# Gate tiles of the selected-key mixer: each behind its own head pair's values, their rounding in one group

## Chip, cores and metric

One Trainium2 chip, one core. The metric is the time on the device in microseconds (us); lower is better. Three runs of the kernel before are given.

## What is computed

The model has two stages for one sequence of 512 positions and width 1024. The first (two layers of convolution, dilated attention, a gated recurrence, and a feed-forward network) is not touched. The second has two layers (l = 0, 1), each of which is cut here to what matters:

```python
z = u @ w_in                                   # u: the normed, modulated input; w_in 1024 x 8772
ya = dsa_attention(rope(aq), rope(ak), av, rope(iq), rope(ik), iw)   # 8 heads of 64; each query keeps the best 128 keys
ya = ya.reshape(bsz, seq, 512) * silu(ag)      # mixer "a": selected keys, gated
yb = swa_sinks_attention(...) * silu(bg)       # mixer "b": window of 128 keys, with sinks
yc = stick_breaking_attention(...) * silu(cg)  # mixer "c"
merged = (sigmoid(ma) * (ya @ w_br_a) + sigmoid(mb) * (yb @ w_br_b) + sigmoid(mc) * (yc @ w_br_c))
x = x + gate * (merged @ w_out)
```

The change concerns `* silu(ag)` in both layers: when its four column tiles are multiplied by TensorE, and when their product with the attention's output is rounded for the next multiplication.

## The kernel before

Activations lie transposed, 128 features on the partitions and all 512 positions along the row. Every large product is made in three fp32 matmuls per 128 x 128 block of weights (line 573, called from `thrice`): high part of the weights by the high and the low part of the input, and low part of the weights by the high part. A chunk of weights (1024 x 256) comes by DMA into one of two buffers `raw` (`sync_program`), ScalarE rounds it into `wh` and VectorE subtracts that from it into `wl`; there are two pairs of those.

The order of all work is one list of units, made in Python before the program is written (`make_order`). Each engine's program walks that list and issues its share of each unit, so all queues run in that order, and semaphores keep the data right. Within a layer of the second stage the list comes from `Order.weave` (line 408): it holds a list of **main** units, which keep their order (tiles of the large products), and several lists of **side** units (attention). At each step it takes a side unit whose conditions are met and whose modelled time has come; otherwise the next part of the main tile in work; and if the next main tile has an unmet condition of its own, only side units. It has a modelled clock per engine (`COST`, `COST_BY_KEYS`), which decides the order and nothing else.

The main units of a layer follow `BLOCK2`. Around the change, for layer 0: ... bkv, bq0, bq1, an0, ag0, ag1, an1, ap0, ap1, am2, am3, bn0, bn1, bn2, bg0, bg1, .... Here `an0` is two tiles of the merge gate of mixer a (`mg`), `ag0` and `ag1` two gate tiles each (`gate`, four in all, c = 0 to 3), `ap` and `am` tiles of `ya @ w_br_a` (`br`) and more merge gates, `bn` merge gates of mixer b, `bg` gate tiles of mixer b. In layer 1 the tiles of bq stand earlier, ahead of mixer c's gates; the rest is the same.

The side units of mixers a and b come from `head_steps` (line 2139), for four head pairs c = 0 to 3 and four query blocks i = 0 to 3 each:

- `s1` scores on TensorE (the rows ps<-ak,aq or ps<-bk,bq), then bias and maximum on VectorE; at most two tiles are in flight (s1 waits for s2 of two tiles before);
- `sx` exponent on ScalarE, `sn` normalizing on VectorE;
- `s2` transposes on TensorE (line 786, ps<-cst_r,s), copied out by ScalarE into `pt`;
- `s3` values on TensorE (ps<-pt,av or ps<-pt,bv), copied by ScalarE over the queries (`aq`, `bq`), which becomes `y`.

Query block i of mixer a looks at i + 1 key blocks, of mixer b at one or two. The sides of mixer b may begin only once `("s3", "a", l, 3, 3)` is done, the last values of mixer a.

A gate tile (`gate`) takes 24 matmuls 128x512 in four parts on TensorE; ScalarE takes tanh into a buffer `rawt` (two of them, `raw_slot`); VectorE makes (tanh + 1) times the tile, and multiplies y by it. That last product waits for `("att", "a", l, c)`. The unit `gs` (`mixer_split`) rounds the gated row: ScalarE writes its high part over the keys `ak` (and waits for the last scores of mixer a, which read them), VectorE writes the low part `aq_r` over y. The tiles `br` need all four rows. The gate tiles of mixer b (`bg`) wait in the planner for the last values of mixer b, `("s3", "b", l, 3, 3)`.

Before, all four gate tiles of mixer a have the condition `("s3", "a", l, 3, 3)`, and `gs` of a tile goes into `late`, which puts it behind the next main tile.

Of the kernel before, what the change touches and what calls it, by code (L numbers as in the profile page):

```python
# [2138 lines left out]
def head_steps(cfg, l, n, first, bias=False):  # L2139

    scores, rest, tiles = [], [], [(c, i) for c in range(n) for i in range(NT)]
    for x, (c, i) in enumerate(tiles):
        if bias and i == 0:
            scores.append((("gb", l, c), [("s1", cfg, l, c - 1, NT - 1)] if c else []))
        after = first(c) + ([("gb", l, c)] if bias else [])
        scores.append((("s1", cfg, l, c, i), after + ([("s2", cfg, l) + tiles[x - 2]] if x > 1 else [])))
        scores.append((("sx", cfg, l, c, i), None))
        rest.append((("sn", cfg, l, c, i), [("sx", cfg, l, c, i)]))
        rest.append((("s2", cfg, l, c, i), None))
        rest.append((("s3", cfg, l, c, i), None))  # L2150
    return scores, rest
# [96 lines left out]
def order_early(o, tag, key, before):  # L2248


    j = o.use(key, True)
    o.put("early", tag, j, 0, 1)
    for k in (KD - 2, KD - 1):
        o.put("sq", norm_before(tag), k)
        o.put("er", tag, k)
    o.put("early", tag, j, 1, KD)
    while o.split_one():
        pass
    o.put("rms", tag)
    o.put("mod", tag, before)  # L2260
    o.put("ed", tag)
    while o.split_one():
        pass
    o.put("em", tag)
    return j


def order_out(o, which, l):
    o.put("banks", (0, 1, 2, 3), (4, 5, 6))
    o.sums()  # L2270
    o.put("lnexp")
    tag, norm = ("o1" if which == 1 else "o3", l), ("m2", l) if which == 1 else ("m3", 1) if l == 0 else ("fin2", 0)
    n, more = 0, norm != ("fin2", 0)
    if more:
        o.put("es", norm)
    for c in range(4):
        j = o.use(("out", which, l, c))
        for os in [(0, 1)] if c == 0 else [(2 * c,), (2 * c + 1,)]:
            o.put("out", which, l, tag, os, j)
            while n < os[-1] and not (more and n == KD - 2):  # L2280
                o.put("sq", norm, n)
                if more:
                    o.put("er", norm, n)
                n += 1
    if not more:
        o.put("sq", norm, n)
# [69 lines left out]
def order_block2(o, l):  # L2356
    j = order_early(o, ("m3", l), ("iq", l), ("o3", 0) if l else ("m2", 1))
    for c in range(2):
        o.put("rope", l, "iq", c, 128 * c, 128, j)
    if l == 0:  # L2360
        o.put("rms", ("fin", 0))
    o.put("banks", (0, 1), (3, 7))
    mains, late = [], [("rest", l, "iq", 0), ("rest", l, "iq", 1)]
    held = [("iw", l), ("rest", l, "ik", 0), ("ikc", l)]
    finals = [("final", ("fin", 0), "fin", k, k + 1) for k in range(KD)] if l == 0 else []
    wide = ("banks", (0, 1, 2), (3, 7, 4, 5, 6))

    def main(units, parts, key=None, after=None):

        mains.append((units, parts, key, after))  # L2370
        while late:
            mains.append(([late.pop(0)], 1, False, None))
        if finals and units[0][0] == "v2":
            mains.append(([finals.pop(0)], 1, False, None))

    def tiles(units, parts, key, after=None):
        for n, unit in enumerate(units):
            main([unit], parts, None if n else key, None if n else after)

    def rope(nm, c, key, n=128, after=None):  # L2380
        main([("rope", l, nm, c, 128 * (c % 2), n)], 4, key, after)
        late.append(("rest", l, nm, c))

    for chunk in BLOCK2[l][1:]:
        nm, x = (chunk[:-1], int(chunk[-1])) if chunk[-1].isdigit() else (chunk, 0)
        if nm in ("cq", "ck"):
            tiles([("cqk", l, nm, 2 * x + c) for c in range(2)], 4, (nm, l, x))
            if held:
                mains += [([held.pop(0)], 1, False, None) for _ in range(3)]
        elif nm in ("cv", "av"):  # L2390
            tiles([("v2", l, nm, x, tb) for tb in range(NT)], 2, (nm, l, x))
        elif nm in ("aq", "ak", "bq"):
            for c in range(2):
                rope(nm, 2 * x + c, (nm, l, x) if c == 0 else None)
        elif nm == "ik":
            main([("rope", l, "ik", 0, 0, 68)], 4, ("ik", l))
        elif nm == "bkv":
            rope("bk", 0, ("bkv", l), after=[("tr", l, 3, 15, 16)])
            main([("bv", l)], 4)
            late += [("bkc", l), ("bvt", l)]  # L2400
        elif nm[1] == "g":
            for c in (2 * x, 2 * x + 1):
                main([("gate", l, nm[0], c)], 4, (nm, l, x) if c % 2 == 0 else None, [wide] if nm == "cg" else [("s3", nm[0], l, 3, 3)])
                late.append(("gs", l, nm[0], c))
        else:
            if nm[1] != "p":
                tiles([("mg", l, nm[0], 2 * x + c) for c in range(2)], 4, (nm[0] + "m", l, x))
            while late and nm[1] == "p":
                mains.append(([late.pop(0)], 1, False, None))
            if nm[1] != "n":  # L2410
                tiles([("br", l, nm[0], 2 * x + c) for c in range(2)], 2, (nm[0] + "br", l, x))

    side_c, side_d = [], []
    steps = [(c, u) for c in range(4) for u in range(3)]
    for n, (c, u) in enumerate(steps):
        side_c.append((("c1", l, c, u), [("cqk", l, "ck", c)] + ([("c2", l) + steps[n - 2]] if n > 1 else [])))
        side_c.append((("ch", l, c, u), [("c1", l, c, u)] + ([("c3", l) + steps[n - 2]] if n > 1 else [])))
        side_d.append((("c2", l, c, u), [("ch", l, c, u)]))
        side_d.append((("c3", l, c, u), [("c2", l, c, u), ("v2", l, "cv", 1, 3)]))
    side_d.append((wide, None))  # L2420
    index, last = [], []
    for i in range(1, NT):
        index += [(("ts", l, i, h), [("ikc", l)] + last) for h in range(4)] + [(("tm", l, i), None)]
        index += [(("tr", l, i, r, r + 1), None) for r in range(16)]
    sides = [side_c, side_d, index]
    for cfg in "ab":
        first = [("tr", l, 3, 15, 16), wide, ("v2", l, "av", 1, 3)] if cfg == "a" else [("bkc", l), ("bvt", l), ("s3", "a", l, 3, 3)]
        sides += head_steps(cfg, l, 4, lambda c, first=first: first)
    o.weave(mains, *sides, ahead=AHEAD2, weight=WEIGHT2, behind=BEHIND)
    order_rows3(o, l)  # L2430
    order_out(o, 2, l)


def order_rows3(o, l):
    for k in range(KD):
        o.put("row", ("o3", l), k)


def make_order(o, first):
    o.put("start")  # L2440
    o.put("adaqp", 0)
    for k in range(KD):
        o.put("sqf", ("m1", 0), k)
    o.put("rms", ("m1", 0))
    for l in range(2):
        order_block1(o, l)
        order_ffn(o, l)
    for l in range(2):
        order_block2(o, l)
    o.put("rms", ("fin2", 0))  # L2450
    o.put("final", ("fin2", 0), "fin2")
    assert o.split == len(o.plan) and not o.late
    return o.units
# [214 lines left out]
```

## Time and profile before

| what | us |
|---|---|
| median of 3 runs | 2777.92 |
| lowest, highest | 2770.64, 4207.18 |
| span of the profiled execution | 2769.2 |
| TensorE busy (matmul records) | 2666.7 |
| VectorE, ScalarE, GpSimd busy | 1855.3, 1153.6, 696.7 |
| layer 0 of the second stage, mixer a's last eight tiles without main work | 34.35 of the span |

No time of its own is listed for the profiled execution beside its span; the lowest run is 1.4 above the span, which is taken for what lies around it. A matmul's record is longer than the distance to the next one, since they are pipelined, so work is read from the distance between the starts. A "granted clock" of 1.00 is 2.4 GHz, 0.50 is 1.2 GHz.

### The profile page before, as it was taken

The numbers are of one execution on the slowest core, as the hardware profiler recorded it, in microseconds if no ns is written. First come the engines' busy times: TensorE is split into PE (matmuls) and PEld (weight loads), VectorE is DVE, ScalarE is ACT, GpSimd is POOL, SyncE is SP. The second block draws the span as 40 slices with busy tenths as digits, with TensorE's granted clock in tenths as the row PEclk, the third lists the DMA queues.
The fourth block names the chain that finished last, engine by engine and source line by source line (L and its number), as shares of the span: only waits on it lengthen the run. The fifth ranks groups of instructions, "written<-read, shape, count | busy, mean of one in ns | idle before, by whom it ended". The sixth has DMA issues, their size and how long they took to land.

```text
span 2769.2 us, 36817 instructions
## 1 busy us (share of the span) xinstructions
PE 2666.7 (96%) x14748; PEld 2135.3 (77%) x14748; DVE 1855.3 (67%) x3088; ACT 1153.6 (42%) x1900; POOL 696.7 (25%) x514
## 2 busy tenths in 40 slices
PE   6999999999999998999999999999999999999997
PEld 5877677888878776787887888776787788777776
DVE  7789668876677775877467868745546548644544
ACT  3243644333242454443224464344434564444432
POOL 0000046998800003365550031000100122000100
PEclk9999999999999998999999999999999999999999
DMA  8443033554432112344442534231223322222322
GB/s 275 123 145 105 30 122 130 168 182 159 153 113 69 60 60 71 121 152 140 149 131 88 179 105 151 84 96 32 91 64 108 96 65 83 88 81 68 94 66 77
DMA packets 281115, 302.58 MB, mean 109 GB/s; under 512 B 9969, under 2 KB 263025, under 8 KB 280945
## 3 DMA queue, kind: packets, MB, share of 16 engines
q1 hardware_dynamic: 267568, 250.21, 29.0%
q0 software_dynamic: 13088, 49.55, 5.4%
q8 instruction: 117, 1.92, 0.3%
q10 hardware_dynamic: 288, 0.47, 0.1%
q14 instruction: 54, 0.43, 0.0%
HBM read 289.97 MB, written 2.10 MB: 105 GB/s over the span
## 4 chain that ended last, share of the span: by engine, by line
PE 85%; DVE 9%; ACT 4%; issue 1%; DMA 1%; SPq 0%; DVEq 0%; ACTq 0%
PE ps L573 82%; PE ps L786 2%; DVE wl L1420 1%; DVE hl L1426 1%; DVE adaacc L1426 1%; DMA raw<-in_w_in 1%; DVE ca L1426 1%; ACT wh L944 1%; DVE recat L1725 0%; ACT hh L944 0%; ACT recat L944 0%; DVE rawt L1426 0%; ACT att_p L944 0%; DVE uv L1426 0%; DMA stage<-in_w_ada 0%
## 5 line engine op out<-in xcount | busy, mean ns | idle before, releaser
L573 PE MATMUL ps<-hh,wh 128*128 128x512 f32 x2208 | 887.4, 402 | 18.8 <-DVE wl L1420 10.7
L573 PE MATMUL ps<-hh,wl 128*128 128x512 f32 x2208 | 864.0, 391 | 0.0
L573 PE MATMUL ps<-hl,wh 128*128 128x512 f32 x2208 | 862.9, 391 | 0.0
L1420 DVE TENSOR_TENSOR wl<-raw,wh 128x2048 fp32r<-128x2048 f32 (+3 forms) x234 | 478.1, 2052 | 143.6 <-ACT wh L944 143.3
L573 PEld LDWEIGHTS ps<-hh,wh 128*128 128x128 f32 x2208 | 414.7, 188 | 133.6 <-issue 40.0
L573 PEld LDWEIGHTS ps<-hh,wl 128*128 128x128 f32 x2208 | 414.9, 188 | 91.2
L573 PEld LDWEIGHTS ps<-hl,wh 128*128 128x128 f32 x2208 | 415.6, 188 | 79.6
L944 ACT ACTIVATE wh<-raw 128x2048 fp32r<-128x2048 f32 (+3 forms) x234 | 370.1, 1592 | 223.4 <-PE ps L573 196.2
L573 PE MATMUL ps<-fh,wh 128*128 128x512 f32 x432 | 172.1, 398 | 2.5 <-DVE wl L1420 2.5
L573 PE MATMUL ps<-fh,wl 128*128 128x512 f32 x432 | 169.0, 391 | 0.0
L573 PE MATMUL ps<-fl,wh 128*128 128x512 f32 x432 | 168.9, 391 | 0.0
L1993 POOL TENSOR_TENSOR strewn<-strewn,cond 128x1024 f32<-128x1024 f32 x80 | 163.5, 2044 | 8.2 <-DMA strewn<-in_w_ada 6.5
L1426 DVE SCALAR_TENSOR_TENSOR xT<-ps,mod,xT 128x512 f32<-128x512 f32 x80 | 59.5, 748 | 135.3 <-PE ps L573 135.2
L1995 POOL TENSOR_TENSOR strewn<-strewn 128x512 f32<-128x512 f32 x84 | 145.6, 1733 | 6.6
L1952 POOL DMA_DIRECT2D gbias<-in_gb x6 | 3.5, 577 | 542.0 <-DVE stt L1423 447.3
L573 PE MATMUL ps<-wh,hh 128*128 128x256 f32 x448 | 128.7, 287 | 3.4 <-DVE apad L1420 3.4
L573 PE MATMUL ps<-wl,hh 128*128 128x256 f32 x448 | 126.7, 283 | 0.0
L573 PE MATMUL ps<-wh,hl 128*128 128x256 f32 x448 | 126.7, 283 | 0.0
L573 PEld LDWEIGHTS ps<-recq,reck 64*128 64x128 f32 x1536 | 100.8, 201 | 26.5 <-issue 14.8
L573 PE MATMUL ps<-recq,reck 64*128 64x64 f32 (+2 forms) x1536 | 110.4, 296 | 5.0 <-DVE reck L1420 3.1
L944 ACT ACTIVATE rawt<-ps 128x512 f32<-128x512 f32 (+1 forms) x82 | 48.7, 597 | 148.4 <-PE ps L573 148.3
L1976 POOL DMA_DIRECT2D strewn<-in_w_ada x80 | 63.1, 788 | 157.6 <-PE ps L573 132.4
(304 smaller groups left out, 4199.3 us busy)
## 6 DMA issues: line engine op xcount, KB each, us to landing
raw<-in_w_in SPq DMA_DIRECT2D x75, 1024.0 KB, 5.3
raw<-in_w_up SPq DMA_DIRECT2D x46, 1024.0 KB, 5.1
strewn<-in_w_ada POOLq DMA_DIRECT2D x80, 512.0 KB, 4.1
raw<-in_w_ada SPq DMA_DIRECT2D x24, 1024.0 KB, 5.3
raw<-in_w_in SPq DMA_DIRECT2D x44, 512.0 KB, 5.1
raw<-in_w_out SPq DMA_DIRECT2D x16, 1024.0 KB, 5.1
raw<-in_w_down SPq DMA_DIRECT2D x16, 1024.0 KB, 5.2
stage<-in_w_ada SPq DMA_DIRECT2D x8, 1024.0 KB, 11.7
```

The source lines that it names most:

```text
L573: return e.matmul(o, a, b, start=start, stop=stop, skip_group_check=True)
L786: m = e.transpose(b[:, o:o + 128], S[:, 128 * x:128 * x + 128], M.ident)
L944: return e.activation(o, a, f, **k)
L1420: return e.tensor_tensor(o, a, b, op)
L1426: return e.scalar_tensor_tensor(out=o, in0=a, scalar=s, in1=b, op0=op0, op1=op1)
L1952: e.dma_start(M.Gb[h], X.T["gb"][2 * c + h, :, :]).then_inc(*X.tally.up16("bias_in", ("bias", l, c)))
L1976: e.dma_start(M.strewn[h][:, :, c:c + n], src[:, 4 * h:4 * h + 4, :]).then_inc(*X.tally.up16(f"strewn_in{h}", ("strewn", j, h)))
L1993: e.tensor_tensor(v, v, weights, ALU.mult).then_inc(*up("pool_ada"))
L1995: e.tensor_tensor(v[:, 0:2, :], v[:, 0:2, :], v[:, 2:4, :], ALU.add).then_inc(*up("pool_ada"))
```

## The change

The planner's condition of gate tile c of mixer a is no longer the last values of the whole mixer but those of its own head pair c, `("s3", "a", l, c, 3)`. The units `gs` of mixer a no longer go one behind each next tile: they are held and put in one group of four behind the fourth gate tile, with the condition `("s3", "a", l, 3, 3)`. Mixers b and c are as before. No instruction is added or removed; only the order of the list differs.

```diff
             for c in (2 * x, 2 * x + 1):
-                main([("gate", l, nm[0], c)], 4, (nm, l, x) if c % 2 == 0 else None, [wide] if nm == "cg" else [("s3", nm[0], l, 3, 3)])
-                late.append(("gs", l, nm[0], c))
+                main([("gate", l, nm[0], c)], 4, (nm, l, x) if c % 2 == 0 else None,
+                     [wide] if nm == "cg" else [("s3", nm[0], l, c if nm == "ag" else 3, 3)])
+                if nm == "ag":
+                    held.append(("gs", l, "a", c))
+                else:
+                    late.append(("gs", l, nm[0], c))
+            if nm == "ag" and x == 1:
+                mains.append(([held.pop(0)], 1, False, [("s3", "a", l, 3, 3)]))
+                mains += [([held.pop(0)], 1, False, None) for _ in range(3)]
```

## Rows read from the trace of the kernel before

**Rows 1.** The page, part 1: busy time of the engines

```profile
PE 2666.7 (96%) x14748; PEld 2135.3 (77%) x14748; DVE 1855.3 (67%) x3088; ACT 1153.6 (42%) x1900; POOL 696.7 (25%) x514
```

**Rows 2.** Stretches: length, busy of each engine, clock, DMA share, GB/s

```profile
1820.43:1857.07 36.64, 36.64 (x201) 27.91 (x200) 20.14 (x48) 17.64 (x39) 5.16 (x4) 1.00 0.39 115
1860.79:1895.14 34.35, 26.00 (x166) 15.45 (x165) 15.27 (x67) 16.88 (x49) 0.00 (x0) 0.75 0.00 1
1895.14:2031.99 136.85, 136.68 (x708) 103.53 (x706) 68.42 (x214) 59.18 (x149) 11.26 (x8) 1.00 0.25 78
2365.00:2506.99 141.99, 141.99 (x770) 107.88 (x768) 71.59 (x175) 62.97 (x133) 4.52 (x3) 1.00 0.26 80
2506.99:2653.67 146.68, 145.28 (x749) 110.74 (x747) 72.15 (x214) 63.20 (x156) 12.20 (x8) 1.00 0.25 79
1867.00:1876.00 9.00, 7.78 (x39) 4.56 (x38) 3.97 (x18) 3.96 (x12) 0.00 (x0) 0.50 0.00 0
```

**Rows 3.** TensorE in time, layer 0, mixer a with main tiles between: start, length

```profile
1842.20 1.13 PE L573 MATMUL ps<-ak,aq 64*128 64x512 f32 x4
1843.26 0.66 PE L573 MATMUL ps<-pt,av 128*64 128x128 f32 x8
1843.85 0.50 PE L573 MATMUL ps<-hh,wh 128*128 128x512 f32 x1
...
1857.07 1.03 PE L786 MATMUL ps<-cst_r,s 128*128 128x128 f32 x8
1857.86 0.48 PE L573 MATMUL ps<-hh,wh 128*128 128x512 f32 x1
```

**Rows 4.** TensorE in time, layer 0, mixer a with no main tile

```profile
1860.79 0.70 PE L573 MATMUL ps<-ak,aq 64*128 64x256 f32 x4
...
1866.55 1.15 PE L786 MATMUL ps<-cst_r,s 128*128 128x128 f32 x4 [1.54 <-DVE s L1423]
1867.63 2.08 PE L573 MATMUL ps<-ak,aq 64*128 64x512 f32 x4
...
1888.13 1.07 PE L786 MATMUL ps<-cst_r,s 128*128 128x128 f32 x6 [1.37 <-DVE s L1423]
...
1894.11 1.09 PE L573 MATMUL ps<-pt,av 128*64 128x128 f32 x16 [0.69 <-ACT pt L944]
1895.14 0.50 PE L573 MATMUL ps<-hh,wh 128*128 128x512 f32 x1
```

**Rows 5.** TensorE's waits from 1860.8 to 1895.2

```profile
PE ps L786 <- DVE s L1423: 6.5, 6, 1.5
PE ps L573 <- ACT pt L944: 1.7, 3, 0.8
```

**Rows 6.** Layer 0: last values of mixer b; ScalarE empties the main tile before gate b

```profile
2031.41 0.66 PE L573 MATMUL ps<-pt,bv 128*64 128x128 f32 x8
...
2033.68 0.60 ACT L944 ACTIVATE ak<-ps 128x512 f32<-128x512 f32 x1 [1.30 <-PE ps L573]
```

**Rows 7.** Layer 1: mixer b's last tile on TensorE

```profile
2646.51 0.70 PE L573 MATMUL ps<-bk,bq 64*128 64x256 f32 x4
...
2651.69 0.70 PE L786 MATMUL ps<-cst_r,s 128*128 128x128 f32 x4 [0.72 <-DVE s L1423]
2653.08 0.66 PE L573 MATMUL ps<-pt,bv 128*64 128x128 f32 x8 [0.69 <-ACT pt L944]
2653.67 0.50 PE L573 MATMUL ps<-hh,wh 128*128 128x512 f32 x1
```

**Rows 8.** VectorE: gate products of mixer b, layer 1, one tile each

```profile
2666.24 0.69 DVE L1420 TENSOR_TENSOR bq<-bq,rawt 128x512 f32<-128x512 f32 x1
...
2671.68 0.69 DVE L1420 TENSOR_TENSOR bq<-bq,rawt 128x512 f32<-128x512 f32 x1
```

**Rows 9.** ScalarE in layer 1: last tile before the gates, gate 0, first rounding

```profile
2515.24 0.60 ACT L944 ACTIVATE cq<-ps 128x512 f32<-128x512 f32 x1 [3.37 <-PE ps L573]
...
2522.37 0.58 ACT L944 ACTIVATE rawt<-ps 128x512 f32<-128x512 f32 x1
...
2531.99 0.61 ACT L944 ACTIVATE ak_r<-aq 128x512 fp32r<-128x512 f32 x1
```

## The prediction

> **What bounds the kernel now.** I read the page's busy times first: TensorE's records cover 96% of the span and no other engine more than 67% [rows 1]. So an order of work pays only where TensorE's share is broken. Next I cut the second stage into stretches and looked where TensorE's busy time falls short of the length [rows 2]. In layer 1 the stretch of mixer a (2365.00 to 2506.99) is full, and that of mixer b lacks 1.4 us in 146.68. In layer 0 mixer b's stretch lacks 0.2 us in 136.85. The one real hole is in layer 0, from 1860.79 to 1895.14: 26.00 us busy in 34.35, with a mean clock of 0.75 and no DMA.
>
> The order of TensorE in time shows what that hole is [rows 4]: between the scores of pair 2, block 1 and the first matmul of gate tile 0 no main tile stands at all. The planner had used up its main tiles, and the next one (gate 0) was held for the last values of mixer a. The waits inside are the attention's own chain: 6.5 us on VectorE's normalizing and 1.7 us on ScalarE's copy of the transposes [rows 5].
>
> **What the hole is worth.** Work at full clock is read from starts in the covered stretch just before [rows 3]: scores of four key blocks take 1843.26 - 1842.20 = 1.06 us, 0.265 a key block; 8 value matmuls take 0.59, 0.074 each; 8 transposes take 0.79, 0.099 each. The hole holds scores over 2+3+4+1+2+3+4 = 19 key blocks (5.0 us), 96 value matmuls (7.1) and 40 transposes (3.9): 16.0 us. So 34.35 - 16.0 = 18.3 us of the hole is excess, in eight tiles of attention, 2.3 us a tile. Of it 8.35 is plain idle time; the other 10 is mostly the low clock: from 1867 to 1876 the granted clock was 0.50, which is 1.2 GHz [rows 2], and the scores that took 1.13 us in the covered stretch took 2.08 [rows 3, 4].
>
> The busy share would say that only those 8.35 us are to be had. The Trainium skill (Perfetto Trace Analysis, Identifying the Most-Contended Engine) says that matmul busy time is a poor measure of a full TensorE, and that the busy time of the weight loads is the better one. By it the covered stretch has 27.91 us of weight loads in 36.64 and the hole 15.45 in 34.35, so the hole holds 20.3 us of work and 14.1 us of excess. That is between my two counts and nearer to the one by starts.
>
> **The change, part by part.**
>
> *Gates 0 and 1 go into the hole.* Their pairs are finished when it begins. A gate tile is 5.44 us of TensorE (distance between two gate products when nothing stands between them [rows 8]), so 10.9 us of main work becomes available. It doesn't slip into idle time alone. With a main tile open the planner puts parts of it between all steps of the attention. From 1820.43 to 1857.07, the transposes of the last blocks of pairs 0 and 1, four tiles of attention took 36.64 us [rows 2], of which their own work is 10 x 0.265 + 40 x 0.074 + 20 x 0.099 = 7.6; so a tile consumes (36.64 - 7.6) / 4 = 7.3 us of main work. Gates 0 and 1 then cover 10.9 / 7.3 = 1.5 tiles.
>
> *Gate 2 goes in too, a little later,* once pair 2's values are done, in the middle of the hole: 5.44 / 7.3 = 0.75 of a tile. Gate 3 waits for the same unit as before. Together 2.25 of the eight tiles get covered and 5.75 stay bare: the gain is 2.25 x 2.3 = 5.2 us. From both sides: if every part fell into a hole and kept the clock up, all of 3 x 5.44 = 16.3 us would be gained (less than the excess of 18.3). If the weight split that comes with each chunk (about 2 us each on ScalarE and VectorE) and the two extra VectorE operations of a gate tile (0.69 each [rows 8]) delay the attention as much as the cover gives, nothing is gained. I take 5.2, since the rate of 7.3 us a tile is what this planner did with the same attention in the same layer.
>
> *Mixer b in layer 0 loses that cover.* The same three tiles were the first main work of mixer b's stretch, 16.3 us of it. Mixer b's attention begins behind the last values of a, as before, and the next fence is bg, which waits for the last values of b. Before, the main tile ahead of gate b ended about 2033.5, when ScalarE took it, 1.5 us behind mixer b's last values (2031.41 + 0.6) [rows 6]. So main tiles now run out 16.3 - 1.5 = 14.8 us too early. Mixer b used up main work at this rate: 136.85 us for 16 tiles [rows 2], a tile's own work being about 1.4 (scores of 1.75 key blocks 0.46, 7 values 0.52, 3.5 transposes 0.35, rounded up for their first loads), leaves 7.1 a tile. So 2.1 tiles of mixer b become bare. The price: layer 1 shows b's last tile nearly bare. From its scores to the end of its values 7.16 us pass (2646.51 to 2653.67), with 2.7 us of main parts and 1.4 us of idle time in it [rows 7]; without those parts about 4.1 us would have been idle. For 2.1 tiles I take 4.1 + 0.5 = 4.6 us. Bounds: 2 us (if mixer b moves faster, since the gate tiles' VectorE work has left its beginning) and 10 us (if the clock falls there as in the hole, 14.8 / 7.1 x 2.3 = 4.8, doubled).
>
> *The group of four roundings.* Nothing is added: four copies on ScalarE (0.61 [rows 9]) and four subtractions on VectorE. But in the new order the fourth follows directly on gate 3. ScalarE's copy must wait for tanh (0.58), the two VectorE products (0.69 each) and then blocks its queue, and VectorE waits in turn for the copy; behind them stand exponents and normalizing of mixer b's first tiles. That is about 2.5 us during which no attention of b advances, and TensorE has a merge-gate tile of 5.44 us in hand. Cost 0 to 2 us a layer; I take 0.5 for both together. The tiles `br`, which need all rows, come two tiles (10.9 us) later, enough.
>
> *Layer 1.* The condition moved doesn't bind there: gate 0 began after ScalarE took the tile ahead of it, about 2515 [rows 9], 8 us behind mixer a's last values at 2506.99. So nothing moves except the roundings. A shift there can change the 1.4 us of idle time at the end of b either way [rows 7]; I take 0.
>
> *DMA, loads and queues.* The splits of ag1 and an1 come some 20 us earlier. SyncE's queue waits for the split before it loads, so loads come earlier as well; the DMA share is 0.00 in the hole, so there is room [rows 2]. No other queue is passed.
>
> **Sum.** -5.2 + 4.6 + 0.5 + 0 = -0.1, and the low clock: the hole's bare pieces are shorter (three tiles at most in a row), so part of its 10 us of low clock may go; I take -1.9 for that. Together -2.0 us. The profiled execution has 2769.2 of span and, by the lowest run, 1.4 around it: 2770.6. The two runs that lie together are 2770.64 and 2777.92; a new median falls between rather than at the lowest, so I count from their middle, 2774.3. Forecast 2772. The point is that the kernel had one supply of main tiles before bg, and the change spends it earlier; the hole moves from the end of mixer a to the end of mixer b, and only the difference in price is won.
>
> **Rivals.**
>
> *The hole is filled and not moved* (-5 to -12 us, about 2765). If the parts fill idle time, 16.3 us are won in mixer a, and the loss in b stays 4.6. For it: TensorE waits in pieces of at most 1.54 us [rows 4], and a part of 1.36 us fits into such a piece. Also, the Trainium skill (same page, Optimization Strategy) advises to interleave stretches with different limits. Against it: the planner spent 7.3 us of main work a tile where 2.3 would do.
>
> *Mixer b is starved at a higher price* (+5 us, about 2779). Place: the end of mixer b in layer 0, just ahead of gate b. The shortage of 14.8 us leaves 2.1 to 2.5 tiles bare with the clock at 0.50 and costs 10 us, while mixer a gains 5.2. It decides from the point where the bare end of b costs more than the hole gives, 5.2. For it: in the hole the clock was at 0.50 by 1867, 6 us behind the last main matmul [rows 2]. Against: mixer b's tiles are short, one or two key blocks.
>
> *The change doesn't do what it says* (0, about 2774). The planner's modelled clock could put all attention of a first, if its units are always due. Against: between 1820 and 1857 it did interleave.
>
> *The grouped roundings stall mixer b in both layers* (+2 to +4, about 2777), by the chain worked out above. That can be told by VectorE's and ScalarE's waits behind gate 3.
>
> **How the numbers follow.** The forecast with its surroundings (-6 to +2) 0.50; filled 0.20; starved 0.12; does nothing 0.08; roundings 0.10. Two in ten left out reach from -11 to +7, so from 2774 the range is 2762 to 2781; it also takes in that the base itself is known to 4 us. 2% of this kernel is 55 us, about what a measurement can tell from no change; all cases lie far inside that. Faster by over 2% gets 0.01, slower 0.01.
>
> **What would show it.** Right: in layer 0 gate matmuls (128x512) stand between scores of pair 2 and 3 of mixer a; the stretch from pair 2, block 1 to the last values grows from 34 to about 45 us, still with about 8 us of idle time or low clock more than the covered stretch; mixer b's stretch shrinks to about 125 us, with 4 to 5 us idle in its last 10. Layer 1's order on TensorE before the gates is the same, and four roundings stand in a row behind gate 3. Wrong: idle time in mixer a's stretch under 3 us (filled), or over 8 us at the end of mixer b (starved), or a change outside layer 0 of the second stage.

## The result: 5 us slower, and the profile after

The changed kernel takes 2779.23 us (median of 20 runs, 2769.56 to 2783.61) against 2772.94 for the kernel before (20 runs). The ratio, in which the one run before of 4207.18 us does not count, is 1.0018, with a 95% interval of 1.001 to 1.0027: about 5 us slower, clear of no change, far inside 2%. The forecast was 2 us faster. The time lies in the stated range; the direction is wrong.

The spans of two profiled executions differ by more (2780.8 and 2769.2), and that difference can't be taken whole: the first scores of mixer a in layer 0, ahead of which no kernel of this study differs, begin anywhere from 1775.6 to 1786.4 us in the traces. So all readings below are distances within one trace, between instructions that every kernel here has. The first, called mixer a's tail, goes from the transposes of pair 1's last block in mixer a, layer 0, to the end of mixer a's last values; the second on to the end of mixer b's last values; the third on to the fourth gate product of mixer b.

| stretch of layer 0, us | before | after | main work moved in or out | gain (+), loss (-) |
|---|---|---|---|---|
| mixer a's last eight tiles | 38.07 | 53.98 | +16.33 (72 matmuls) | +0.4 |
| mixer b | 136.85 | 126.38 | -14.97 (66) | -4.5 |
| to the fourth gate product | 24.81 | 24.67 | -1.36 (6) | -1.2 |
| sum | 199.73 | 205.03 | 0 | -5.3 |

The six matmuls of the third row are the part of the main tile ahead of gate b that ran behind mixer b's last values before. Mixer b and the row behind it lose 5.7 us together. The 1.2 us behind mixer b are low clock: the granted clock is 0.95 there and was 1.00, and the first matmuls behind the bare end stand 0.43 us apart where 0.23 is usual.

From the fourth gate product of layer 0 to the end of mixer a in layer 1 it is 450.2 us in both, and from there to layer 1's fourth gate product 170.1 in both. The 5.3 us are the whole effect in the traces, and they agree with the ratio.

The same view of stretches as [rows 2], of the kernel after: mixer a's tail, mixer b in layer 0, mixer b in layer 1, and two pieces of mixer a's tail (length, busy of each engine, clock).

```profile
1863.48:1917.46 53.98, 46.44 (x257) 32.77 (x256) 23.78 (x76) 23.66 (x57) 0.00 (x0) 0.80 0.06 20
1917.46:2043.84 126.38, 122.82 (x642) 92.32 (x640) 62.63 (x205) 54.42 (x144) 10.29 (x8) 0.99 0.24 76
2518.68:2665.34 146.66, 145.25 (x748) 110.71 (x746) 71.76 (x214) 63.29 (x156) 12.20 (x8) 1.00 0.25 79
1887.00:1892.00 5.00, 4.98 (x30) 3.69 (x28) 1.79 (x9) 2.84 (x10) 0.00 (x0) 0.50 0.00 0
1904.00:1920.00 16.00, 13.45 (x64) 8.87 (x63) 3.82 (x14) 5.72 (x15) 0.00 (x0) 0.50 0.01 1
```

Mixer a's tail is still 7.5 us short of busy, though 16.3 us of work went in; its clock is 0.80, where the same eight tiles had 0.78 before. Mixer b in layer 0, nearly full before, now lacks 3.6. Layer 1 is as it was.

TensorE's waits in mixer a's tail after, against [rows 5] (who waited for whom, total, times, longest):

```profile
PE ps L786 <- DVE s L1423: 6.2, 3, 2.5
PE ps L573 <- ACT pt L944: 1.4, 2, 0.7
```

Three waits for VectorE's normalizing add up to nearly what six did before. TensorE in time shows where the longest two stand, and ahead of them a tile that did not wait.

```profile
1874.43 0.38 PE L786 MATMUL ps<-cst_r,s 128*128 128x128 f32 x2
...
1876.13 0.92 PE L573 MATMUL ps<-ak,aq 64*128 64x384 f32 x4
1876.98 0.44 PE L573 MATMUL ps<-pt,av 128*64 128x128 f32 x4
1877.35 0.50 PE L573 MATMUL ps<-hh,wh 128*128 128x512 f32 x1
...
1880.21 0.60 PE L786 MATMUL ps<-cst_r,s 128*128 128x128 f32 x4
1880.57 0.48 PE L573 MATMUL ps<-hh,wh 128*128 128x512 f32 x1
...
1882.13 0.66 PE L573 MATMUL ps<-pt,av 128*64 128x128 f32 x8
1882.72 1.13 PE L573 MATMUL ps<-ak,aq 64*128 64x512 f32 x4
1886.28 1.54 PE L786 MATMUL ps<-cst_r,s 128*128 128x128 f32 x6 [2.43 <-DVE s L1423]
...
1895.55 0.38 PE L786 MATMUL ps<-cst_r,s 128*128 128x128 f32 x2
1895.69 0.48 PE L573 MATMUL ps<-hh,wh 128*128 128x512 f32 x1
...
1899.99 0.44 PE L573 MATMUL ps<-pt,av 128*64 128x128 f32 x4
1900.36 0.92 PE L573 MATMUL ps<-ak,aq 64*128 64x384 f32 x4
1903.81 1.15 PE L786 MATMUL ps<-cst_r,s 128*128 128x128 f32 x4 [2.53 <-DVE s L1423]
```

In the two groups with the long waits, read from above: transposes of a tile, gate matmuls (6 in the first, 18 in the second), values, scores of the tile two further on, and only then the wait. Nothing of the gate is left to stand in it. The tile at 1874.43 is of the same size as the one at 1895.55 and also has 18 gate matmuls, but 12 of them stand behind its scores and values (from 1877.35), and the next transposes (1880.21) follow without a wait.

What VectorE does ahead of the last of these waits, the one that ends at 1903.81 (bias and maximum of the scores from 1900.36, then normalizing of the tile that TensorE waits for):

```profile
1900.73 0.69 DVE L1426 SCALAR_TENSOR_TENSOR rawt<-rawt,ps 128x512 f32<-128x512 f32 x1 [1.96 <-ACT rawt L944]
1901.45 0.69 DVE L1420 TENSOR_TENSOR aq<-aq,rawt 128x512 f32<-128x512 f32 x1
1902.06 0.55 DVE L1764 CUSTOM_DVE_ANT_0 s<-ps,sel 128x384 f32<-128x384 f32 x1
...
1903.40 0.35 DVE L1423 TENSOR_SCALAR s<-s,stt 128x256 f32<-128x256 f32 x1
```

So the normalizing comes behind the newest scores, and the two products of a gate tile stand ahead of both. At the end of mixer b the last two tiles are bare, with 3.5 us of waits (forecast: 2.1 tiles, 4 to 5 us idle):

```profile
2037.29 0.70 PE L573 MATMUL ps<-bk,bq 64*128 64x256 f32 x4
2038.04 0.66 PE L573 MATMUL ps<-pt,bv 128*64 128x128 f32 x8
2041.52 0.70 PE L786 MATMUL ps<-cst_r,s 128*128 128x128 f32 x4 [2.82 <-DVE s L1423]
2042.91 1.00 PE L573 MATMUL ps<-pt,bv 128*64 128x128 f32 x8 [0.69 <-ACT pt L944]
```

### The profile page after: what moved, and what is told of

Read it like the earlier page. It is cut to its first block, busy times and chain, and to the rows that moved or that the text cites. A ratio compares the mean times of both kernels' runs of the same rounds, so it can differ in the third digit from the quotient of the medians.

```text
span 2780.8 us, 36816 instructions
## 1 busy us (share of the span) xinstructions
PE 2675.6 (96%) x14748; PEld 2143.2 (77%) x14748; DVE 1856.2 (67%) x3088; ACT 1154.0 (41%) x1900; POOL 697.7 (25%) x514
## 4 chain that ended last, share of the span: by engine, by line
PE 85%; DVE 9%; ACT 3%; issue 1%; DMA 1%; SPq 0%; DVEq 0%; ACTq 0%
PE ps L573 83%; PE ps L786 2%; DVE wl L1420 1%; DVE hl L1426 1%; DVE adaacc L1426 1%; DVE ca L1426 1%; DVE recat L1725 1%; DMA raw<-in_w_in 0%; ACT wh L944 0%; DVE rawt L1426 0%; ACT recat L944 0%; DMA stage<-in_w_ada 0%; DVE uv L1426 0%; ACT hh L944 0%; DVE reck L1420 0%
## 6 DMA issues: line engine op xcount, KB each, us to landing
stage<-in_w_ada SPq DMA_DIRECT2D x8, 1024.0 KB, 11.6
```

## The experiments

The three stretches of layer 0 for every kernel, read in its one trace between the same instructions. The kernels e1, e2, e4, e8, e11 and e12 ran once each, so for them there is no comparison of whole times:

| kernel | mixer a's tail | mixer b | to gate product 4 | sum |
|---|---|---|---|---|
| before | 38.07 | 136.85 | 24.81 | 199.73 |
| after | 53.98 | 126.38 | 24.67 | 205.03 |
| e1 group only | 37.08 | 137.71 | 24.81 | 199.60 |
| e2 two gates | 47.42 | 133.34 | 24.44 | 205.20 |
| e4 short vector | 51.82 | 125.94 | 25.90 | 203.66 |
| e5 spare, after | 53.46 | 125.71 | 25.31 | 204.48 |
| e6 spare, before | 35.52 | 136.88 | 24.80 | 197.20 |
| e7 own pair b, after | 53.88 | 133.39 | 12.57 | 199.84 |
| e8 own pair b, before | 37.03 | 137.83 | 24.80 | 199.66 |
| e9 = e8 + spare | 35.52 | 136.86 | 24.80 | 197.18 |
| e10 = e7 + spare in bare tiles | 50.88 | 132.18 | 12.57 | 195.63 |
| e11 = e12 + e4 | 50.08 | 125.69 | 24.99 | 200.76 |
| e12 spare in bare tiles, after | 50.87 | 125.71 | 24.75 | 201.33 |
| e13 parts in the waits | 40.10 | 128.85 | 25.17 | 194.12 |
| e14 = e13 + own pair b | 40.11 | 135.43 | 12.57 | 188.11 |

(e3 moves other work through these stretches and is read below.)

**Which part of the change costs.** e1 keeps the grouped roundings and undoes the condition:

```diff
-                     [wide] if nm == "cg" else [("s3", nm[0], l, c if nm == "ag" else 3, 3)])
+                     [wide] if nm == "cg" else [("s3", nm[0], l, 3, 3)])
```

> Only the grouped roundings of the change; the gate tiles wait for all of mixer a, as before. Measure: layer 0, from the transposes of pair 1's last block (mixer a) to the last gate product of mixer b: 199.7 us before, 205.0 after. If the whole loss comes from the moved condition, this run shows 199.7 (within 0.3) and the same 38.1 us for mixer a's last eight tiles. If the grouped roundings stall mixer b, it shows 201 to 203, with new waits of TensorE behind gate 3.

Measured: 199.60, the kernel before. Mixer a's tail took 37.08 here and 37.03 in e8, which both have the TensorE order of the kernel before in it, against 38.07 there; mixer b took 0.9 more. So the sums are the safer number, and the tail of a single trace is good to 1 us. Against these two tails the change's +0.4 in mixer a would be -0.6, and its loss behind it 4.7: nothing was gained in mixer a, by either reading. The roundings cost nothing.

e2 lets only gates 0 and 1 go ahead (`c if nm == "ag" and c < 2 else 3`).

> The change, but only gates 0 and 1 may go ahead of mixer a's end; gates 2 and 3 wait for its last values. Theory cheap tiles and low clock (the price of a bare tile is not 2.3 us for each; cover put on short blocks saves little, and bare rows of tiles left cost more at 1.2 GHz): mixer a's stretch (38.1 before, 54.0 after, of which 16.3 are the three gates) is 38.1 + 10.9 - 1 = 48, and mixer b's end loses a third less, so the whole stretch is 201.5 to 203. Rival, the even price of my prediction: mixer a's stretch 38.1 + 10.9 - 3.5 = 45.5, the whole 199 to 200.

Measured: mixer a's tail 47.42, so the 10.9 us of gates 0 and 1 gained 1.5 there (0.5 against the tails of e1 and e8). The third gate tile then gained nothing: it adds 6.56 to the tail and is 5.44 long. The sum, though, is 205.20, as bad as with three gates and over the range that I gave: 10.9 us of main work are taken out behind mixer a, 9.5 of them (42 matmuls) from mixer b's stretch, and only 3.9 us are saved, 3.5 of them in mixer b. That is a loss of 7.0, where three gates lost 5.7. The price at the end of b doesn't go by how much cover is missing. The planner spent what was left faster: the last main part began about 10 us ahead of the end of b's values, and about 8 us with three gates. Here the granted clock was 0.97 in b's stretch (0.99 after), and the last group of four transposes, at 2032.76, took 1.12 us where 0.60 is usual. The stretch:

```profile
1902.36:2035.70 133.34, 129.65 (x666) 97.53 (x664) 65.21 (x209) 56.58 (x147) 13.19 (x8) 0.97 0.24 76
```

**Is mixer b's loss the missing supply?** e3 puts the two tiles bn3 ahead of bg:

```diff
-           "bn0", "bn1", "bn2", "bg0", "bg1", "bn3", "bp0", "bp1", "bp2", "bp3")] * 2
+           "bn0", "bn1", "bn2", "bn3", "bg0", "bg1", "bp0", "bp1", "bp2", "bp3")] * 2
```

> The change, and the last two merge-gate tiles of mixer b (bn3, 10.9 us of main work) put ahead of the gate tiles bg in both layers, so that mixer b's end has cover again. Theory (the loss in mixer b is the missing supply of main tiles ahead of bg): the 3.5 us idle at the end of b in layer 0 fall under 1 and those in layer 1 (1.4) to 0; against the kernel after 4 to 6 us less, so about equal to the kernel before or 1 below. Rival (the work moved forward is missed further back, or the planner spends it earlier just the same): idle time stays at 3 to 4 us, or appears ahead of the tiles bp, and the time is that of the kernel after.

Measured: ratio to the kernel before 0.9997 (0.9985 to 1.0009), so level with it. The idle time at the end of b went from 3.5 to 0 in layer 0 and from 1.4 to 0 in layer 1. With bn3's 10.9 us taken off, layer 0's sum is 199.9. But behind the gates, where bn3 had stood, time is lost: the way to layer 1's mixer a is 1.9 us longer (bn3 taken off), and so is the end of layer 1 by 1.8. Both theory and rival hold in part.

e7 gives mixer b's gates the same own-pair condition (`c, 3)` for all), on top of the change; e8 does that to the kernel before.

> The change, and the gate tiles of mixer b too wait for their own pair's values only, in both layers (their roundings stay where they are). Supply theory: mixer b's end is covered by its gates 0 to 2, so its stretch in layer 0 loses 4 to 5 us against the kernel after (idle 3.5 to under 1), layer 1 loses its 1.4; whole kernel level with the kernel before, within 2 us. Rival: the gates of b are spent in the same way and leave the last tiles bare again, idle at the end of b stays above 2 us.

> The kernel before with mixer b's gate tiles behind their own pairs. Layer 0 has cover to the end of b before, so its stretches stay (199.7 us); layer 1 loses the 1.4 us idle at the end of b. If more changes, the gates' condition has a price or gain of its own.

Measured: e7 0.9995 (0.9984 to 1.0006), and its mixer b in layer 0 has no gap left:

```profile
1910.64:2044.03 133.39, 133.39 (x690) 100.99 (x688) 66.14 (x208) 57.30 (x147) 10.29 (x8) 0.99 0.24 76
```

Its sum is 199.84, with mixer a's tail as in the kernel after (53.88), so 5.2 of the 5.3 us are back, and layer 1 gains 1.7 (168.43 for 170.12). e8 leaves layer 0 alone (199.66) and gains the same 1.7 in layer 1. The loss in mixer b was the missing supply of main tiles ahead of bg.

**Why mixer a gained nothing: VectorE, clock, or place.** e4 shortens VectorE's work of the gates and the weights' rounding:

```diff
+            if p["key"] in (("ag", 0, 1), ("am", 0, 1)):
+                c1 = c0 + 16
...
+        n = 16 if l == 0 and nm == "a" and c < 3 else 512
-        tt(y, y, raw, ALU.mult).then_inc(*up("dve_gate", ("gated", l, nm, c)))
+        tt(y[:, 0:n], y[:, 0:n], raw[:, 0:n], ALU.mult).then_inc(*up("dve_gate", ("gated", l, nm, c)))
```

> The change, but in layer 0 the VectorE products of gate tiles 0 to 2 and the rounding of the weights of ag1 and an1 work on 16 columns only (most of these values are left out); order and waits stay. Theory VectorE in the way (gate products of 0.69 us each and a split of 2.3 stand in the queue ahead of the attention's maximum and normalizing): TensorE's waits of 2.4 and 2.5 us in mixer a's stretch fall to 1.5 or less and the stretch from 54.0 to 50 to 51.5. Rival (low clock and cheap tiles only): the stretch stays at 53 to 54.

Measured: 51.82, 2.2 us less; the waits for VectorE fell only from 6.2 to 5.3, the longest to 2.2. That is a part of the loss; the stretch ends just over the 50 to 51.5 of the theory. By the sum it is 1.4 us less (203.66), since the stretch to the fourth gate product took 25.90 for 24.67.

e5, e6 and e12 add spare matmuls so that TensorE's clock stays up:

```diff
+    def spare(cfg, l, c, b, n):
+        if cfg == "a" and l == 0 and c > 1:
+            for _ in range(n):
+                mm(b[:, :], M.cst_r[:, C_ID:C_ID + 128], M.hh[:, 0, :], True, True)
```

> The change, and in layer 0 for pairs 2 and 3 of mixer a spare matmuls (128x512, fp32r, into the bank just claimed, whose content the next instruction overwrites) ahead of the waits: 5 before a tile's transposes (1 for the first block), 2 before its values. They add no result. Theory low clock (the bare tiles of the kernel after cost more since they run at 1.2 GHz): the granted clock stays at 1.00 through mixer a's stretch, which falls from 54.0 to 48 to 50 us, and mixer b's first main part is no longer slow. Rival (bare tiles are bound by VectorE and ScalarE, and the clock costs little): the stretch stays at 53 to 55, since TensorE has to wait for them all the same.

> The same spare matmuls in the kernel before. Low clock theory: mixer a's last eight tiles take 30 to 33 us and not 38.1, so this kernel gains 5 us or more, which says how much of the hole was the clock's. Rival: 37 to 39.

> The change, with the spare matmuls (5 ahead of the transposes, 2 ahead of the values) only in the five tiles of layer 0 that stand bare in it: pair 2, blocks 2 and 3, and pair 3, blocks 1 to 3. In the run with spare matmuls in all tiles mixer a's stretch was 53.5 us, with some 13 spare matmuls (3 us) among covered tiles. If the low clock is a part of the lost gain, the stretch is now 50 to 51 (54.0 without). If those 3 us were hidden before too and the clock is worth nothing, 53 to 54.

Measured: e5 53.46, as its rival had it; e6 35.52, between theory and rival; e12 50.87, as by its theory. The clock did stay up; the tail of e6 and of e12:

```profile
1855.28:1890.80 35.52, 34.81 (x233) 22.73 (x231) 15.28 (x67) 17.80 (x51) 0.00 (x0) 1.00 0.00 1
```

```profile
1853.90:1904.77 50.87, 48.08 (x292) 33.46 (x291) 23.80 (x76) 23.06 (x57) 0.00 (x0) 1.00 0.07 21
```

So the low clock was worth 2.5 us in the kernel before (I had booked up to 10 of its hole to it, and expected 5 here) and 3.1 in the kernel after (by the sums 2.5 and 3.7). In e5 the 13 spare matmuls among covered tiles cost 2.6 us of their own, the difference to e12. Over whole executions e6 is a little faster than before, 0.9987 (0.9976 to 0.9998); e5 is slower, 1.0025 (1.0014 to 1.0036).

> Both at once: the spare matmuls in the five bare tiles, and the VectorE products of gates 0 to 2 and the weights' rounding for ag1 and an1 on 16 columns (left out for most values). VectorE alone gave 51.8 us for mixer a's stretch. If clock and VectorE add up, 48 to 49, which is near what my even price gave (38.1 + 16.3 - 5.2 = 49.2); what is then missing to the 35.5 + 16.3 = 51.8 of the kernel before with spare matmuls is the true cover of the gates, 3 us or so. If they are one and the same loss, 50 to 51.

Measured: 50.08. Clock (3.1) and VectorE (2.2) don't add up: together they give 3.9. With the clock kept up on both sides, 35.52 + 16.33 = 51.85 is what no cover at all would give; the three gate tiles cover 1.0 us of their 16.3 (e12), 1.8 with short VectorE work as well, about what two traces can differ by. What was left open is why main work in a stretch full of waits hides in none.

e13 moves nothing into or out of layer 0 and changes the order within mixer a's tail: where the parts of gates 0 to 2 stand, how many stand together (one a tile, but two in the first), and that scores always come ahead of values, as in the kernel before. One tile of it, as a list of units and not as code:

```diff
 s2(2,3), s1(3,1), s3(2,3)
+part of gate 1
 sx(3,1), sn(3,0), s2(3,0), s1(3,2), s3(3,0)
+part of gate 1
 sn(3,1), sx(3,2), s2(3,1)
-(planner: part, s2(3,0), part, part, part, s3(3,0), s1(3,2), sn(3,1), s2(3,1))
```

> The change, but in layer 0 the list of mixer a's last eight tiles is written by hand: the attention in the order of the kernel before, and ten of the twelve parts of gates 0 to 2 one by one behind a tile's scores and values, ahead of the next transposes, where TensorE waits for VectorE. Theory place (in the kernel after, the parts stand ahead of scores(t+2), which VectorE works through before it normalizes tile t+1, so they lengthen the loop that TensorE waits on and do not fill the wait): with the parts behind the scores most of their 13.6 us are hidden; the whole stretch of layer 0 is 194 to 199 us (205.0 after, 199.7 before). Rival (attention with cover takes that long wherever the parts stand, because VectorE's extra work and the quantum of 1.4 us cost it): 203 to 206.

> The same, and mixer b's gates behind their own pairs. By the theories place and supply together the loss at the end of b (5 us) goes too: layer 0 189 to 194 us, layer 1 1.7 less; 7 to 11 us less than before, ratio 0.996 to 0.9975. If only supply holds: 199 to 200 and 1.7, ratio 0.999.

Measured: e13 0.9981 (0.997 to 0.9993), e14 0.9967 (0.9955 to 0.9978). The tail holds ten gate parts (60 matmuls, 13.6 us) and takes 40.10 us, 2.0 more than the kernel before without them: 11.6 us are hidden, and the clock is at 1.00 without a spare matmul. Against the kernel before with the clock kept up (e6, 35.52) 9.0 us are hidden; the rest is what the clock gives back.

```profile
1857.40:1897.50 40.10, 37.77 (x245) 25.06 (x243) 20.23 (x72) 20.58 (x54) 0.00 (x0) 1.00 0.05 14
```

```profile
1883.83 0.92 PE L573 MATMUL ps<-ak,aq 64*128 64x384 f32 x4
1884.68 0.44 PE L573 MATMUL ps<-pt,av 128*64 128x128 f32 x4
1885.05 0.50 PE L573 MATMUL ps<-hh,wh 128*128 128x512 f32 x1
...
1886.31 0.40 PE L573 MATMUL ps<-hh,wl 128*128 128x512 f32 x1
1886.66 0.90 PE L786 MATMUL ps<-cst_r,s 128*128 128x128 f32 x4
```

These are the same transposes that waited 2.53 us in the kernel after. Scores and values go first, the gate's part follows, and they start right behind it. The sum, 194.12, is in the theory's range. e14 has the better of both: 188.11 in layer 0, a little under the forecast, and 1.7 less in layer 1. By its trace it is 13.3 us below the kernel before, by whole executions about 9 (6 to 12.5 by the interval); why the trace shows more stays open. Its ratio is the lowest here.

> The kernel before, mixer b's gates behind their own pairs, and spare matmuls in pairs 2 and 3 of mixer a in layer 0. By the two looks: 2.5 us from layer 0 (197.2 for 199.7) and 1.7 from layer 1, 4 us less than before, ratio 0.9985. If they disturb one another, under 2 us.

> The change, mixer b's gates behind their own pairs too, and spare matmuls in the five bare tiles of mixer a. With supply at the end of b and the clock kept up, the gates' cover is a net gain: layer 0 is 196 to 197 us (199.7 before), layer 1 1.7 less; 4.5 to 5.5 us less than before, ratio 0.998. If the cover of the gates gains nothing even then, 2 to 3 us less than before, and the kernel before with both additions is the faster.

Measured: e9 0.9986 (0.9975 to 0.9998), e10 0.998 (0.9968 to 0.9992), in the traces 4.2 and 5.8 us less than before. e9 is as forecast, e10 gains a little more than its forecast (195.63 in layer 0 for 196 to 197). By these two traces the change as the planner lays it out is worth 1.6 us once supply and clock are put right; the intervals of the whole executions overlap, so that is not shown beyond noise.

## Why the prediction was wrong, step by step

- **Where the effect is.** Right: only layer 0, from mixer a's tail to the end of mixer b. Layer 1 takes the same 170.1 us, since its condition never bound.
- **"Together 2.25 of the eight tiles get covered ... the gain is 2.25 x 2.3 = 5.2 us."** This is the step that failed: it measured 0.4, and 1.0 with the clock kept up. The step has an even price in it, an excess of 2.3 us a tile that disappears with any main work of 7.3 us a tile. Taking the main matmuls (0.227 us each) out of the distances from one tile's transposes to the next shows what happened. From blocks (2,0) to (2,1) the rest fell from 3.48 to 1.70 us, and from (1,3) to (2,0) from 3.28 to 2.78. But from (3,0) to (3,1), with 18 gate matmuls in it, all ahead of the scores, it rose from 3.48 to 4.18: the main work there came on top. The pair (2,0), (2,1) had as many, 12 of them behind the scores. Low clock isn't what sets the two apart: in e12, with the clock at 1.00, (3,0) to (3,1) took the same 8.26 us. From (2,3) to (3,0), with 6, the rest rose from 3.51 to 4.12 too, but there the part stood behind the scores. That place had only 0.5 us of waits to fill before, and at a clock of 0.50 the eight transposes took 1.97 us where they had taken 1.29.
- **The reason, by e13.** The static order has a loop: TensorE's scores of tile t+2 go to VectorE, whose queue has their maximum ahead of normalizing tile t+1, and TensorE's transposes of t+1 wait for that. A part put between the transposes of t and the scores of t+2 makes this loop longer; the same part behind the scores stands in the wait. The planner places a part as soon as nothing is due by its model, which was the wrong side for 48 of the 84 main matmuls in the tail. The runs show that the order within the tail decides. e13 changed three things in it at once (place, spread, scores ahead of values), and no run tells them apart; within the kernel after, the two pairs of tiles with 18 gate matmuls each speak for place, and the values that came ahead of the scores there are only 0.4 us of work. That the loop is closed by VectorE's order is read from the list and from VectorE's rows (1902.06, 1903.40), and wasn't tried by exchanging maximum and normalizing. The gate products ahead of the maximum (1900.73, 1901.45) are a smaller part: with them cut short (e4) this pair took 7.62 us for 8.26.
- **What the hole is worth.** The busy records left 8.35 us free, and e13 hid 11.6 of the 13.6 us that it put into the same tiles (10.6 against the tails of e1 and e8, 9.0 beyond what the clock gives back). So the busy share did understate the room. The Trainium skill (Perfetto Trace Analysis, Identifying the Most-Contended Engine) warns that matmul busy time is a poor measure of a full TensorE, and this trace agrees. Whether its 14.1 us by weight loads or my 18.3 by starts is the true size isn't shown, since no run put in more. That 10 us of the excess were "mostly the low clock" was wrong: keeping the clock up gave 2.5 (e6).
- **The loss at the end of mixer b, 4.6 us.** Right in kind and near in size: 4.5 in mixer b's stretch and 1.2 right behind it, 5.7 together. Of that, 3.3 us are added waits, all in the last two tiles, 1.2 the low clock behind them, and about 0.6 low clock carried over from mixer a (the first gate part behind it took 2.8 us for 1.4, and e12 loses 5.1). The rate (2.1 tiles) can't be trusted in general: e2 lost 7.0 for less cover.
- **"-1.9 for the low clock."** Wrong sign. The bare pieces were shorter, yet from 1904 to 1920 the clock was 0.50 for 16 us on end, longer than at any place of mixer a's tail before. In the kernel after the low clock costs 3.1 us in the tail where it cost 2.5, and 1.2 more behind mixer b.
- **Roundings, 0.5.** 0.1 or less (e1).
- **The rival "starved at a higher price"** (+5, about 2779, given 0.12) named the outcome and the place, but its reason was only half of it: it had mixer a gain 5.2 and b lose 10. The rival "filled" was possible with this supply, but not by this planner; e13 and e14 are that case.

My sum balanced two large terms, each with an error of its own size, and booked the last 1.9 us from no row. The rate of 7.3 us a tile (by count it is 30 main matmuls, 6.8 us) came from a stretch in which TensorE was full (36.64 us of 36.64 [rows 2]), so it says how fast the planner spends main work and not how much of a wait a part fills. Taking the one for the other is what made the price even.

## What to carry to other kernels

Main work that is moved to a hole helps only if it stands on the instruction that waits; put ahead of an instruction that feeds the loop, it was paid in full here. So list, between two waits, what stands before and after the producer. When a fence is loosened early in a fixed supply of filler, look at the next fence for the same hole, and loosen both.

## What the runs showed of the hardware

In the kernel before, TensorE was busy by its records for 3.60 of the 5.21 us from 1860.79 to 1866.00 and then in a wait of 1.54 us, the longest of that tail; there the granted clock fell from 1.00 to 0.50, where it stayed until about 1876. In e13 ten parts of six matmuls stood in the same tiles, one wait of 1.49 us was left, and the clock stayed at 1.00. The price of the low clock is far below what the doubled durations suggest. A group of four score matmuls takes 2.08 us for 1.13, and the mean clock of mixer a's tail was 0.78 before, so about 17 of its 38.07 us were at 0.50; keeping the clock up was still worth only 2.5 us, of the 18.3 us of excess. Most of what the matmuls lost must have stood in time that TensorE would have waited anyway. Where nothing waits the price is full: behind mixer b's bare end in the kernel after, the first matmuls stood 0.43 us apart for 0.23, and 1.2 us were lost.
